# Three products of 256 columns for each tile of weights, and units scaled straight from PSUM

## What is computed

```
h = rms_norm(x, norm1_w)
proj = h @ w_in
x = x + (g_nsa * (o_nsa @ w_up_nsa) + g_dn * (o_dn @ w_up_dn)) @ w_o
h2 = rms_norm(x, norm2_w)
x = x + (silu(h2 @ w_ffn_gate) * (h2 @ w_ffn_up)) @ w_ffn_down     # 5632 wide
x = rms_norm(x, norm_f_w)
h = rms_norm(x, attn_norm_g_2)
proj = h @ w_in_2
x = x + concat(y_rwkv, y_mla) @ w_out_2
h = rms_norm(x, ffn_norm_g_2)
x = x + (silu(conv3(h @ w_gate) + b) * (h @ w_up)) @ w_down
return rms_norm(x, final_norm_g_2)
```

## Time and profile before

| | before |
|---|---|
| runs | 2802.66, 2800.72, 2800.12 us |
| median | 2800.72 us |
| the profiled execution | 2797.75 us |
| its span in the trace | 2795.9 us |
| mean granted clock of TensorE | 0.998 of full speed |
| busy: TensorE, its loads, VectorE | 2754.8, 2431.0, 2012.8 us |
| busy: ScalarE, POOL | 1370.3, 484.0 us |
| HBM read | 469.87 MB, 169 GB/s over the span |

### The profile page before, as it was taken

The page is one execution under the profiler, slowest core; times in us unless marked ns, Lnnn a source line. Parts: engine busy times, 40 slices in busy tenths (PEclk is TensorE's granted clock), DMA queues, the critical chain, the costliest instruction groups (busy, mean ns, idle before and its releaser), DMA issues.

```text
span 2795.9 us, 42233 instructions
## 1 busy us (share of the span) xinstructions
PE 2754.8 (99%) x16660; PEld 2431.0 (87%) x16660; DVE 2012.8 (72%) x3057; ACT 1370.3 (49%) x2059; POOL 484.0 (17%) x526
## 2 busy tenths in 40 slices
PE   8999999999999999999999999999999999999998
PEld 7888888888888888888888888888998888888887
DVE  7987897776766666656657889868677777667655
ACT  6453555455554554444436545533554444444434
POOL 2221111100111111001102633620111111001001
PEclk9999999999999999999999999999999999999999
DMA  6544334455555555555556433321465555555555
GB/s 225 166 158 159 128 130 151 150 188 189 191 188 193 188 191 194 189 191 193 190 181 211 160 106 120 106 76 61 149 199 192 192 189 191 193 189 192 193 179 160
DMA packets 133396, 474.72 MB, mean 170 GB/s; under 512 B 14800, under 2 KB 15056, under 8 KB 132944
## 3 DMA queue, kind: packets, MB, share of 16 engines
q1 hardware_dynamic: 133200, 472.02, 51.4%
HBM read 469.87 MB, written 2.10 MB: 169 GB/s over the span
## 4 chain that ended last, share of the span: by engine, by line
PE 87%; DVE 8%; ACT 2%; POOL 1%; issue 1%; DMA 0%; SPq 0%; DVEq 0%; ACTq 0%; POOLq 0%
PE ps L957 86%; DVE ringl L1942 3%; DVE U L1942 3%; POOL U L2613 1%; DVE U L1951 1%; ACT high L1468 1%; PE ps L960 0%; DVE U L1948 0%; DVE xT L1942 0%; DVE U L2137 0%; DMA xT<-in_x_dram 0%; POOL U L2686 0%; DVE U L2225 0%; DVE hx L1942 0%; DVE U L2146 0%
## 5 line engine op out<-in xcount | busy, mean ns | idle before, releaser
L957 PE MATMUL ps<-hr,high 128*128 128x512 f32 x4672 | 1490.1, 397 | 12.1 <-DVE ringl L1942 11.0
L1942 DVE TENSOR_TENSOR ringl<-ring,high 128x1024 fp32r<-128x1024 f32 x888 | 1086.5, 1226 | 438.2 <-ACT high L1468 437.6
L1468 ACT ACTIVATE high<-ring 128x1024 fp32r<-128x1024 f32 x888 | 915.5, 1033 | 615.8 <-PE ps L957 602.8
L957 PEld LDWEIGHTS ps<-hr,ringl 128*128 128x128 f32 x4672 | 879.3, 188 | 192.4 <-issue 0.7
L957 PE MATMUL ps<-hr,ringl 128*128 128x256 f32 x4672 | 924.0, 279 | 0.0
L957 PEld LDWEIGHTS ps<-hr,high 128*128 128x128 f32 x4672 | 718.4, 188 | 21.1 <-issue 14.8
L957 PE MATMUL ps<-yur,high 128*128 128x512 f32 (+1 forms) x2432 | 681.0, 369 | 2.9 <-issue 1.6
L2613 POOL TENSOR_TENSOR U<-U,rs 128x256 f32<-128x256 f32 x292 | 272.9, 935 | 1651.7 <-DVE U L1942 1632.4
L957 PEld LDWEIGHTS ps<-yur,ringl 128*128 128x128 f32 x2176 | 399.3, 188 | 80.4 <-issue 0.7
L1468 ACT ACTIVATE U<-ps 128x256 f32<-128x256 f32 (+4 forms) x481 | 173.7, 372 | 573.1 <-PE ps L957 556.6
L957 PE MATMUL ps<-yur,ringl 128*128 128x256 f32 x2176 | 429.1, 279 | 0.0
(11 more groups left out here) (179 smaller groups left out, 1239.8 us busy)
## 6 DMA issues: line engine op xcount, KB each, us to landing
ring<-in_w_dram SPq DMA_DIRECT2D x862, 512.0 KB, 3.3
ring<-in_w_dram SPq DMA_DIRECT2D x48, 256.0 KB, 3.4
xT<-in_x_dram SPq DMA_DIRECT2D x3, 512.0 KB, 8.5
out_dram<-hx SPq DMA_DIRECT2D x3, 512.0 KB, 2.7
cst<-in_cst_dram SPq DMA_DIRECT2D x1, 1438.5 KB, 13.0
yT<-in_lora_dram SPq DMA_DIRECT2D x1, 1024.0 KB, 7.8
xT<-in_x_dram SPq DMA_DIRECT2D x2, 256.0 KB, 5.0
U<-in_lora_dram SPq DMA_DIRECT2D x1, 512.0 KB, 5.5
```

Of the source, the lines that this page charges most:

```text
L957: return e.matmul(out, l, r, start=start, stop=stop)
L1468: return e.activation(out, i, ACT.Copy, scale=scale)
L1942: return e.tensor_tensor(out, a, b, op)
```

## The change

Every unit now does what `wout` did: for each k-tile three products of 256 columns into the left half of the bank. `halves`, `both`, `rest` and the buffer `um` are gone. A unit then falls in one of three kinds. `by_vector`: VectorE reads the bank and multiplies by `rs` (or adds into x, or multiplies the gate) in one instruction, which frees the bank and is the data's last step; ScalarE and POOL do nothing. `scaled_later`: the first two units of the kernel and all of `lora`, `rw` and `lat`, where ScalarE copies the left half and frees the bank, and POOL multiplies by `rs`. The rest (`cmpkc`, `vs`, `uv`, `uq` and the like) stay with ScalarE as they were. The waits for a buffer to be free move with the step from ScalarE to VectorE, and who waited for POOL's "sc" now waits for VectorE's "free". VectorE's step waits for TensorE (`used`), no longer for ScalarE's half. The planner's tables follow.

```diff
-TILE, TILE4, TILE33, ROWS = 0.346, 0.432, 0.23, 0.70
+TILE, TILE4, TILE33, ROWS = 0.341, 0.432, 0.23, 0.70
...
+        def by_vector(u):
+
+            return u.kind not in ("cmpkc", "cmpvc", "vs", "vw", "uv", "uq", "uk") and not scaled_later(u)
+
+        def scaled_later(u):
+            return u.i < index[("dn", 0, 0, 1)] or u.kind in ("lora", "rw", "lat")
...
-                            c = mact if one_half(prev) else mdve
+                            c = mdve if by_vector(prev) else mact
                             e.wait_ge(c.sem, c.after("free", prev.i))
...
-                                if u.kind == "wout":
-                                    for n_, half in enumerate(moving(u, k0 + k)):
-                                        mm(out[:, 0:SEQ], wh, half, start and n_ == 0, False)
-                                else:
-                                    mm(shaped(out[:, :], 2, SEQ), wh, halves(u, k0 + k), start, False)
-
+                                for n_, half in enumerate(moving(u, k0 + k)):
+                                    mm(out[:, 0:SEQ], wh, half, start and n_ == 0, False)
                                 for j in (k, k - 1) if k % 2 else ():
...
             def evac0(u):
 
                 src, key = ps[u.bank][:, 0:SEQ], u.key
-                if u.kind in ("down", "wout", "wo"):
+                if by_vector(u):
...
-                copy(place_of(u), src).then_inc(mact.sem, mact.inc("free" if one_half(u) else "half", u.i))
+                copy(place_of(u), src).then_inc(mact.sem, mact.inc("free", u.i))
...
-            def rest(u, dst):
-
-                e.wait_ge(mact.sem, mact.after("half", u.i))
-                tt(dst, dst, ps[u.bank][:, SEQ:2 * SEQ], ADD).then_inc(mdve.sem, mdve.inc("free", u.i))
-
...
+                if u.i in FIRSTS:
+                    e.wait_ge(mpe.sem, mpe.after("first", u.i))
+                else:
+                    e.wait_ge(used.sem, used.after(u.end()))
...
-                        stt(mixT[:, t, :], s, 1.0, um[:, t % 2, :], ADD, MUL).then_inc(mdve.sem, mdve.inc("sg", t))
+                        stt(mixT[:, t, :], s, 1.0, src, ADD, MUL).then_inc(mdve.sem, mdve.inc("free", u.i))
+                        mdve.also("sg", t)
...
+                    if u.i in SUMS:
+                        e.wait_ge(mdve.sem, mdve.after("rs", SUMS[u.i]))
+                    tt(place_of(u), src, rs, MUL).then_inc(mdve.sem, mdve.inc("free", u.i))
+                    return
...
-                    parts = 1 if u.kind == "wout" else 2
-                    for j in range(parts):
-                        src = ps[u.bank][:, SEQ * j:SEQ * j + SEQ]
-                        if u.kind == "wo":
-                            i = stt(x, src, 0.5, x, MUL, ADD)
-                        else:
-                            i = tt(x, x, src, ADD)
-                        i.then_inc(mdve.sem, mdve.inc("free", u.i) if j == parts - 1 else mdve.inc())
...
+                if u.kind == "wo":
+                    i = stt(x, src, 0.5, x, MUL, ADD)
+                else:
+                    i = tt(x, x, src, ADD)
+                i.then_inc(mdve.sem, mdve.inc("free", u.i))
...
-                if normed(u):
-                    e.wait_ge(mdve.sem, mdve.after("free", u.i))
+                if scaled_later(u):
+                    e.wait_ge(mact.sem, mact.after("free", u.i))
```

More of the change, by code:

```diff
@@ L847, in build @@
             ends = p.ends.get(m - 1, [])
-            own = [u for u in ends if not sums_x(u)]
-            both_ = [u for u in ends if not one_half(u)]
+            own = [u for u in ends if not by_vector(u)]
+            then = [u for u in ends if by_vector(u)]
+            scaled = [u for u in ends if scaled_later(u)]
             later = [u.kind for u in p.ends.get(m - 2, [])]
@@ L858, in build @@
                     work["DVE"].append((m - 0.75, 0.0, [], []))
-            own, then = [u for u in own if u in ends[-1:]], [u for u in both_ if u in ends[-1:]]
+            own, then = [u for u in own if u in ends[-1:]], [u for u in then if u in ends[-1:]]
             work["ACT"].append((m - 0.5, COPY * (len(own) + later.count("mg") + later.count("up")), [("end", u.i) for u in own] + [("data", u.i) for u in p.ends.get(m - 2, []) if u.kind == "mg"],
[L861 to L864, removed]
+                                [("free", u.i) for u in own] + [("data", u.i) for u in own if not scaled_later(u)], "exp" if mixed else None))
+            work["DVE"].append((m - 0.5, JOIN * (len(then) + later.count("up")),
+                                [("end", u.i) for u in then], [("free", u.i) for u in then] + [("data", u.i) for u in then]))
+            work["POOL"].append((m - 0.5, SCALE * len(scaled), [("free", u.i) for u in scaled], [("data", u.i) for u in scaled]))
             work["POOL"].append((m, 0.0, [("used", m - 1)] if 0 < m <= M else [], []))
@@ L1486, in root @@
                 if before is not None:
-                    e.wait_ge(mpool.sem, mpool.after("sc", before))
+                    c, name = (mpool, "sc") if scaled_later(units[before]) else (mdve, "free")
+                    e.wait_ge(c.sem, c.after(name, before))
                 e.activation(rtmp if tag == "attn_g" else rs, ps[7][:, 0:SEQ], ACT.Sqrt, scale=1.0 / DM, bias=C("eps"))\
@@ L1536, in evac0 @@
                     return
[L1538 to L1563, removed]
-                    e.wait_ge(gpe.sem, gpe.after("gl"))
-                elif u.kind == "lora":
+                if u.kind == "lora":
                     e.wait_ge(mpool.sem, mpool.after("pads"))
@@ L1995, in evac0 @@
                         mdve.also("sg", 16 + t)
-                elif u.kind in ("wo", "down", "wout"):
-                    x = xT[:, key[-1], :]
-                    if u.i in FIRSTS:
-                        e.wait_ge(mpe.sem, mpe.after("first", u.i))
-                    else:
-                        e.wait_ge(used.sem, used.after(u.end()))
-                    if u.kind == "wout" and key[0] == 0:
-                        e.wait_ge(ldve.sem, ldve.after("xs", key[1]))
-                    parts = 1 if u.kind == "wout" else 2
-                    for j in range(parts):
-                        src = ps[u.bank][:, SEQ * j:SEQ * j + SEQ]
-                        if u.kind == "wo":
-                            i = stt(x, src, 0.5, x, MUL, ADD)
-                        else:
-                            i = tt(x, x, src, ADD)
-                        i.then_inc(mdve.sem, mdve.inc("free", u.i) if j == parts - 1 else mdve.inc())
-                        if j < parts - 1:
-                            e.wait_ge(mdve.sem, mdve.last())
-                    if summed_in(u) not in ("", "final_g") and key[-1] == 15:
-                        low_of(summed_in(u), 15)
-                else:
-                    rest(u, place_of(u))
@@ new lines, in evac0 @@
+                x = xT[:, key[-1], :]
+                if u.kind == "wout" and key[0] == 0:
+                    e.wait_ge(ldve.sem, ldve.after("xs", key[1]))
+                if u.kind == "wo":
+                    i = stt(x, src, 0.5, x, MUL, ADD)
+                else:
+                    i = tt(x, x, src, ADD)
+                i.then_inc(mdve.sem, mdve.inc("free", u.i))
+                if summed_in(u) not in ("", "final_g") and key[-1] == 15:
+                    low_of(summed_in(u), 15)
@@ L2297, in rope @@
                 def rope(buf, key, last):
-                    e.wait_ge(mpool.sem, mpool.after("sc", last))
+                    e.wait_ge(mdve.sem, mdve.after("free", last))
                     for a in (0, 64):
```

68 lines of the change are left out of this document (39 added, 29 removed).

## The result

The changed kernel took 2838.05 us (median of 4 runs, 2837.68 to 2838.82) against 2801.69 us for the kernel before beside it (4 runs, 2800.12 to 2804.99): ratio 1.0129, 95% interval 1.0111 to 1.0146. It is slower by 36 us. The forecast was 2765 us, the range ended at 2790, and 0.10 was given to slower.

The account below looks back on a forecast made before the run. TensorE, busy 2754.8 of 2795.9 us, was taken as the bound. Gains of 24 + 2 + 4 + 3 + 2.4 + 0.4 = 36 us took the profiled 2797.75 to 2762, forecast median 2765 us; range 2748 to 2790.

Parts of the forecast that it names:

- Step (1): All TensorE products: three 256-column matmuls replace 512 + 256, 0.340 us a k-tile against 0.345; 24 us in quiet stages.
- a gain of 0 to 8 us: The two recurrence stages: 1608 k-tiles at up to 5 ns gained each; the middle, 4 us, taken.
- The 2 us for `up`: Some 170 k-tiles of the two `up` matrices outside the recurrence stages: 10 ns each gained if separate halves reach 0.34 us.
- rival A: Gain stays in the quiet stretches, none in recurrence stages or `up`: 2778 or 2790 us; chance 0.22.
- Rival B: Quiet stages run at the slow 0.70 us a pair, weight loads lacking slack: 2820 us; chance 0.12.
- (2): Scaled units: VectorE's 418 ns product from PSUM replaces its add; ScalarE loses 110 us, POOL 238; direct worth 0.
- (4): Last lot of `down`, first FFN: one sum fewer in eight units, 2.9 us, of which 2.4 counted here.
- (3): `lora`, `rw`, `lat`, `gates`, first `dn`: VectorE's add falls away, 15 us of its time; 3 us gained, bounds 0 to 10.
- (5): Planner's new places for side steps between the engines' main work: -4 to +4 us, taken as 0.
- The ring of the last lot: VectorE and ScalarE chain in the last `down` lot, first FFN: 4.49 us a unit, forecast to fall to 4.13.
- the end: After the last matmul, one sum less: 0.4 us gained.
- Rival C: VectorE's evacuation becomes the bound and TensorE waits for banks: 2775 to 2795 us, 2800 at worst; chance 0.08.

Follow-up runs that it names:

- experiment 7: Kernel before with its 512-column product split in two of 256, old evacuation kept, gap of 112 words: 2782.65 us (median of 10).
- experiment 1: Kernel before with only its 512-column product split in two of 256 columns, old evacuation kept: 2837.99 us, ratio 1.0128.
- the lower group: Six of ten runs of the changed kernel with a gap of 112 words instead of 16: 2768 to 2774 us; the other four 2804 to 2807.
- experiment 3: Changed kernel with only the gap ahead of the moving data changed from 16 words to 0, 32, 64, 96, 112 or 120: 2774.41 to 2888.04 us.

## Why the prediction was wrong

**Step (1) failed**, and with it the sign. It took 0.340 us a k-tile for all quiet stages from the part of w_out behind 1998 us, "the long undisturbed run", and explained the 0.70 us a pair at 1978 us as unsettled. It even misread that row: 0.70 us is longer than the old form's 0.69, a loss and not "hardly better", so the same rows held both a gain and a loss, and the stages with the long step should not have been given a gain of 0 to 8 us. Both paces were steady. The trace of before shows the switch between them, and it is a pause:

```profile
1985.58 0.63 PE L957 MATMUL ps<-yur,high 128*128 128x256 f32 x4
...
1988.02 0.70 PE L957 MATMUL ps<-yur,high 128*128 128x256 f32 x4 [1.57 <-issue]
```

Up to 1986 us w_out runs 0.70 us a pair where nothing else stands between (once 0.68, at 1981 us); behind the 1.57 us stop, 0.68, to its end. In the changed kernel the stop at this place, also 1.57 us, left the long step as it was. The window of the earlier trace rows began ten microseconds behind that stop. Which pace 4984 k-tiles of other stages would have, no row of before could say. In the changed kernel the merge gates and `wo` got the short step and the FFNs the long one: in the two FFNs 353.3 ns where I had 340, and 13.3 ns for each of the some 3900 k-tiles of the third and sixth stretch are 52 us of the miss of 77 between the two profiled executions. By stages, in the quiet ones forecast and result lie 60 us apart (-28.8 against +30.9), in the stretch to 604 us and the second recurrence stage 17 (-7 against +10.2).

In the first mixed stage, where I took a gain from "both paces occur", the long step held too: 10.4 us more for 1312 k-tiles, 8 ns each. The 2 us for `up` came to nothing: of the stretch 614 to 818 us only merge gates and `wo` run at 0.68, `up` at 0.70 as before. Two slips of the sum did not matter: 51 us below 2801 is 2750, not 2748, and the range ends at 2790 where rival A's band ends at 2792.

The rule of the Trainium skill that I had set aside ("TensorE: Matmul & The Clock Gate", section "Back-to-back issue gap", a fixed 2.5 ns beyond the columns, which the page gives as the gap of a single matmul by itself, with other figures and none for 256 columns for a stream of loads and matmuls) had the sign right, and by an estimate from it the change loses 16 us. The trace does not bear out its size or that it is one number: beyond 106.7 ns for 256 columns a product took 6.6, 11.1 or 13.3 ns by place and pace.

**Rival B** is what happened, at a chance of 0.12 and a price of 5 ns; the price was 8.3 against the old form and it applied in the mixed stages too, so 2838 and not 2820. That its price was too small has the same root, a pace read from starts rounded to 0.01 us. Its reason, loads not far enough ahead, is open: the loads are busy without a break at 113.3, 117.8 and 120.0 ns alike, and only the small effect of placement on the old form speaks for it.

**Steps (2) and (4) held; (3) and (5) can't be told apart.** VectorE's new step is as priced, and POOL has 37 products with `rs` left:

```profile
L1895 DVE TENSOR_TENSOR U<-ps,rs 128x256 f32<-128x256 f32 x255 | 107.8, 423 | 96.8 <-PE ps L951 96.4
...
L2584 POOL TENSOR_TENSOR U<-U,rs 128x256 f32<-128x256 f32 x37 | 35.0, 946 | 128.6 <-ACT U L1447 108.3 <-DVE rs L1895 14.1 <-DVE rs L1915 6.2
...
L1447 ACT ACTIVATE U<-ps 128x256 f32<-128x256 f32 x57 | 21.8, 382 | 75.1 <-PE ps L951 73.3 <-POOL yT L2584 1.6
```

ScalarE's copies fell from 344 to 57, by the 287 counted, and their time by 110 us; its total fell by 89 only (the split of the weights took 5 us more, the rest I did not follow). The ring of the last lot went from 35.06 to 32.51 us, 2.6 less where 2.9 were forecast, and is now TensorE's own pace (busy 32.51 of 32.51). Together (3), (4), (5) and the end were put at 5.8 us; experiment 7 measures 7 to 9 where the products run as assumed, experiment 1 nothing at the long step. There the new evacuation won 1.7 us in the last lot and 1.5 in the second recurrence stage against experiment 1's profile and lost 2.3 before 604 us, which single executions may differ by. Rival C (the evacuation as the bound) is out by TensorE's idle time. Rival A did not occur.

At the place where the short step is to be had, the sum nearly comes out: 2773 us in the lower group against 2765. By the trace at 2774.41 us the quiet stages won 27 us of the 28.8; the mixed ones lost 4 where 7 were to be won, as both steps occur there, at 116 ns a product on average.

## What to carry to other kernels

A pace read from one stretch of a trace is the pace of that stretch: if the same form shows two values, look for what switches between them before taking either, and price both over the whole kernel. When a product is split so that a weight load stands behind every 256 columns, the time can go by where the moving data lie in SBUF (2774 to 2888 us here), so a change of the product's form is compared at the best placement of each form: of the three tried for the old form, gap 16 was its best. The changed kernel with a gap of 112 words beats both kernels in the median (2774 against 2803 us), but four runs in ten give that gain back.

## What the runs showed of the hardware

- The start-to-start time of a 256-column fp32r product with a load of its own was 120.0, 118.7, 118.3, 117.8 or 113.3 ns by the gap between weights and moving data, modulo 128 words (the table of experiment 3). The weights were never moved, so that the distance counts, and not the moving data's own place, is not shown, nor what the two reads might share. The Trainium skill ("SBUF — State Buffer", section "SBUF: two separate sides") has TensorE wait for no other engine's access to SBUF. The runs don't speak against that; what they show is a dependence of its pace on the place of its own moving operand.
- At gaps of 16 and 112 words there are two paces for the same instructions and operands, 113.3 and 117.8 ns a product. Each keeps itself for hundreds of microseconds. At 16 words four float32 products switched it from the short to the long one, at 112 they did not. A stop of 1.57 us led from long to short in one trace and left the long one in another; stops of 0.56 us worked in both directions or not at all. In the changed kernel it went from long to short without a stop, over two units whose operands lie elsewhere (597 to 603 us). Short probes met only the long pace and did not switch it. What picks the pace is open.
- The 512-column form showed no second pace in fourteen pauses, and moves by 3 ns a k-tile between gaps of 16, 64 and 112 where the split form moves by 20.
